# A turned merge, a freed buffer as a ring place, and a small router table ahead of the rest of the router

## The reference, cut to what matters

```python
y_r, y_n = rwkv7_time_mix(...), nsa_mix(...)                 # each 512 tokens x 512
gates  = sigmoid(zg).reshape(B, T, 2, D)
merged = gates[:, :, 0] * (y_r @ p_rwkv) + gates[:, :, 1] * (y_n @ p_nsa)
h  = h + gt1 * (merged @ w_out)
u2 = rmsnorm(h, norm_ffn_g) * (1 + sc2) + sh2
# router: best group of 4, two best of its 8 experts, weights from both softmaxes
# experts: every expert's tokens, in blocks;  hid = silu(x @ w_gate[e]) * (x @ w_up[e]);  hid @ w_down[e]
h  = h + gt2 * hier_moe(u2, ...)
return rmsnorm(h, norm_final_g)
```

## Time and profile before

| | us |
|---|---|
| time, median of 3 runs | 1168.78 (1166.61 to 1171.31) |
| profiled execution, time | 1164.38 |
| profiled execution, span | 1162.5 |
| PE busy | 1064.9 (92%) |
| DVE busy | 474.9 (41%) |
| ACT, POOL busy | 203.0, 161.3 |
| DMA, mean over the span | 258 GB/s |

### The profile page before, as it was taken

How to read it: one execution, slowest core, us unless ns; L and a number is a source line. 1 busy time by engine, 2 the same in 40 slices (tenths; PEclk the granted TensorE clock), 3 DMA queues, 4 the chain that set the end, 5 groups by cost and what they waited for, 6 DMA issues and landing times.

```text
span 1162.5 us, 13892 instructions
## 1 busy us (share of the span) xinstructions
PE 1064.9 (92%) x5547; PEld 512.2 (44%) x5547; DVE 474.9 (41%) x831; ACT 203.0 (17%) x444; POOL 161.3 (14%) x225
## 2 busy tenths in 40 slices
PE   5999999999998898998999859999999989989796
PEld 4443344455445565776444524443333333333332
DVE  4663446563082653457424451122222313212165
ACT  4011114332102564232101200000000000000003
POOL 4100001141200444212000010100000000000321
PEclk8999999999999999999999979999999989999999
DMA  9933427324936300100874489999999999999993
GB/s 351 385 108 109 162 92 283 116 90 154 253 107 157 109 1 23 44 3 2 339 278 184 161 320 402 426 429 425 429 425 427 427 428 426 426 427 426 426 401 128
DMA packets 73377, 299.62 MB, mean 258 GB/s; under 512 B 21422, under 2 KB 27920, under 8 KB 60384
## 3 DMA queue, kind: packets, MB, share of 16 engines
q1 hardware_dynamic: 59776, 278.00, 60.7%
q0 software_dynamic: 6912, 15.46, 3.5%
q10 hardware_dynamic: 6624, 5.26, 1.5%
HBM read 288.13 MB, written 17.84 MB: 263 GB/s over the span
## 4 chain that ended last, share of the span: by engine, by line
PE 43%; DMA 4%; DVE 2%; issue 2%; ACT 1%; SPq 0%; POOLq 0%; ACTq 0%; DVEq 0%
PE ps L2776 18%; PE ps L2802 9%; PE ps L2693 5%; PE ps L2754 5%; DMA ring<-in_moe_w_down_dram 3%; PE ps L2644 3%; PE ps L2737 1%; PE ps L2786 1%; ACT hdT L2268 1%; PE ps L2660 1%; PE ps L2875 1%; DMA zrT<-u_dram,slots 0%; DVE mg L2601 0%; PE ps L2672 0%; PE ps L2632 0%
## 5 line engine op out<-in xcount | busy, mean ns | idle before, releaser
L2776 PE MATMUL ps<-ring,zrT 128*64 128x512 f32 x624 | 189.6, 608 | 14.8 <-issue 13.9
L1058 PE MATMUL ps<-ring,uT 128*128 128x512 f32 x384 | 169.9, 597 | 0.6 <-PE ps L976 0.6
L2776 PEld LDWEIGHTS ps<-ring,zrT 128*64 128x64 f32 x624 | 60.5, 140 | 135.8 <-issue 135.8
L1047 PE MATMUL ps<-uT,ring 128*128 128x512 f32 x256 | 116.2, 611 | 2.0 <-DVE uT L709 1.4
L2802 PE MATMUL ps<-ring,hdT 128*64 128x512 f32 x336 | 99.2, 594 | 12.7 <-ACT hdT L2268 11.4
L1058 PEld LDWEIGHTS ps<-ring,uT 128*128 128x128 f32 x384 | 71.4, 190 | 86.8 <-issue 86.3
L2484 DVE TENSOR_TENSOR cst<-cst,ps 128x512 f32<-128x512 f32 x16 | 11.0, 688 | 167.5 <-PE ps L2776 167.5
L1047 PEld LDWEIGHTS ps<-uT,ring 128*128 128x128 f32 x256 | 49.0, 195 | 66.1 <-issue 64.8
L2517 DVE TENSOR_TENSOR h<-h,ps 128x512 f32<-128x512 f32 x64 | 44.0, 688 | 61.3 <-PE ps L2754 60.6
L2496 DVE TENSOR_TENSOR zrT<-ps,mod 128x512 f32<-128x512 f32 x32 | 22.1, 692 | 99.2 <-PE ps L2802 99.2
L2802 PEld LDWEIGHTS ps<-ring,hdT 128*64 128x64 f32 x336 | 33.2, 137 | 65.6 <-issue 65.6
(11 more groups left out here) (446 smaller groups left out, 1447.7 us busy)
## 6 DMA issues: line engine op xcount, KB each, us to landing
ring<-in_moe_w_gate_dram SPq DMA_DIRECT2D x19, 2048.0 KB, 34.4
ring<-in_moe_w_up_dram SPq DMA_DIRECT2D x18, 2048.0 KB, 35.2
ring<-in_moe_w_down_dram SPq DMA_DIRECT2D x18, 2048.0 KB, 35.4
ring<-in_w_in_dram SPq DMA_DIRECT2D x8, 2048.0 KB, 12.5
ring<-in_w_ada_dram SPq DMA_DIRECT2D x8, 2048.0 KB, 8.6
ring<-in_w_ada_dram SPq DMA_DIRECT2D x16, 512.0 KB, 13.4
zrT<-in_moe_w_gate_dram SPq DMA_DIRECT2D x4, 2048.0 KB, 35.8
zrT<-in_moe_w_up_dram SPq DMA_DIRECT2D x3, 2048.0 KB, 38.5
```

What stands on the lines that cost most here:

```text
L1047: ins = pe.matmul(ps[:, n % 4, :], slot(name, KD, w)[:, k, c0:c0 + P], uT[:, k, :], start=(k == 0), stop=(k == KD - 1))
L1058: ins = pe.matmul(ps[:, n % 4, :], uT[:, k, P * i:P * i + P], w, start=(k == 0), stop=(k == KD - 1))
L2776: ins = pe.matmul(ps[HALF * r:HALF * r + HALF, "gu".index(kind), :], xgT[:, k, HALF * r:HALF * r + HALF], w[r][:, k, :], start=(k == 0), s ...
```

## The change

Merge: the products are made the other way round (weights held still, tokens streamed), so that they come out already turned; DVE writes `mgT` at once, eight tiles of 128 columns by 512 tokens, and `mg`, its transposes and ACT's copies are gone. `gates_dram` is stored turned too, and the gate loads become eight of 0.5 MB, the later four after `m_mg` 1 to 4. The two p_nsa products of tiles 6 and 7 move ahead of the wait for y_r's transposes. `mg`'s room becomes `tenth`, ring place 7, first in `order`, with no condition. Place 6 now waits for the four rows in memory, since the second half of the `u2` buffer lies in it. Place 0 is given back after the first output product.

Router: DVE makes a small table of the 16 pairs alone (`at_expert`, `at_rank`, 16 small products, `r_pt`), from which come the first 16 `slots`. The rest of the router follows, with DVE's copy `tokens(0)` put in its middle. The large table (`tables`) is made after product g of pair 0, the weights' table (`weight_table`) in the middle of its product u.

```diff
-        ztiles += [("zg", f"zg{b}{j}", i, 0) for j in range(2) for b in range(2) for i in range(NT)]
+        ztiles += [("zg", f"zg{b}{j}", i, P * i) for j in range(2) for b in range(2) for i in range(NT)]
-                        if kind == "T":
+                        if kind in ("T", "zg"):
...
-        order = (1, 2, 0, 9, 5, 3, 4, 6, 7, 8)
+        order = (7, 1, 2, 0, 9, 5, 3, 4, 6, 8)
...
                 elif turns == 0 and s_ == 6:
-                    eng.wait_ge(n2_u, NT)
-                elif turns == 0 and s_ == 7:
                     eng.wait_ge(n2_row, 16 * NT)
...
-                else:
+                elif (turns, s_) != (0, 7):
                     eng.wait_ge(unit_free[s_], turns + fills[s_])
...
+                def gate(n):
+                    wait(sp, m_mg, n - 3)
+                    sp.dma_start(gates[:, n % 4, :, :], gates_dram[:, P * n:P * n + P, :].rearrange("b p n -> p b n"))\
+                        .then_inc(m_gt[n % 4], 16)
+
+                for n in range(4):
+                    gate(n)
                 load_units(sp, index["wo0"], index["wo1"])
-                sp.wait_ge(m_mg, 2)
-                gate(2)
+                gate(4)
+                gate(5)
                 load_units(sp, index["wo1"], NU)
-                sp.wait_ge(m_mg, 4)
-                gate(3)
+                gate(6)
+                gate(7)
                 sp.dma_start(h[:, :, :], ...)
...
@@ DVE, merge @@
-                    dve.tensor_tensor(mg[:, i, cols], tmps[:, 0, :], tmps[:, 1, :], ALU.add).then_inc(m_mg, 1)
+                    dve.tensor_tensor(mgT[:, n, :], tmps[:, 0, :], tmps[:, 1, :], ALU.add).then_inc(m_mg, 1)
...
@@ DVE, router, after ohb @@
+                TS(at_expert[:, :, :, 0:NPAIR], oh_half, C("place"), None, ALU.mult).then_inc(r_ex, 1)
+                for j in range(2):
+                    TT(at_expert[:, NT * j:NT * j + NT, :, NPAIR:], oh_half[:, NT * j:NT * j + NT, :, :], ...)
+                dve.wait_ge(r_rk, 1)
+                link(TT(t64[:, :, :, :], oh[:, :, :, :], over_both(ps[:, 1, 0:NT * E]...), ALU.mult))
+                link(dve.tensor_reduce(R_, t64[:, :, :, :], AX, ALU.add))
+                TT(at_rank[:, :, :], C("iota")[:, 0:HALF]..., rx..., ALU.is_equal).then_inc(r_ra, 1)
+                link(dve.tensor_copy(cnt[:, :], ps[:, 1, NT * E:NT * E + E]))
+                link(TS(M_, R_, float(HALF), None, ALU.is_ge))
+                dve.wait_ge(r_pt, 1)
+                link(TS(hi[:, 0:NPAIR], ps[:, 2, NPAIR:2 * NPAIR], -float(P), float(T), ALU.mult, ALU.add))
+                dve.tensor_tensor(slots[:, 0:NPAIR], hi[:, 0:NPAIR], ps[:, 2, 0:NPAIR], ALU.add).then_inc(r_sl, 1)
...
+                tokens(0)
...
                 dve.tensor_copy(w_part[:, 2, :, :], w_blk[:, :, :]).then_inc(r_wp, 1)
+                dve.wait_ge(r_tab, 1)
+                link(TS(hi[:, :], ps[:, 2, NBLK:2 * NBLK], -float(P), float(T), ALU.mult, ALU.add))
+                link(dve.tensor_tensor(slots[:, NPAIR:NBLK], hi[:, NPAIR:NBLK], ps[:, 2, NPAIR:NBLK], ALU.add))
...
@@ PE, merge @@
-                def turned(m):
...
+                for n in (6, 7):
+                    nsa_product(pe, n, n - 2)
+                pe.wait_ge(m_yTe, NT)
+                for n in range(KD):
+                    if n >= 4:
+                        pe.wait_ge(m_mg, n - 3)
+                    for k in range(4):
+                        ins = pe.matmul(ps[:, n % 4, :], slot("p_rwkv", 4, D)[:, k, P * n:P * n + P], yrT[:, k, :],
+                                        start=(k == 0), stop=(k == 3))
+                    ins.then_inc(m_p, 1)
...
@@ PE, output product @@
+                            if n == 0:
+                                pe.wait_ge(m_mg, k + 1)
...
+                        if n == 0:
+                            pe.sem_inc(unit_free[0], 1)
...
@@ PE, router and experts @@
+                for n in range(2 * NT):
+                    for half in range(2):
+                        ins = pe.matmul(ps[HALF * half:HALF * half + HALF, 2, 0:2 * NPAIR], at_rank[:, n, :],
+                                        at_expert[:, n, half, :], start=(n == 0), stop=(n == 2 * NT - 1))
+                ins.then_inc(r_pt, 1)
...
                     for k in range(KD):
+                        if (kind, b, k) == ("u", 0, 4):
+                            weight_table()
...
                     product("g", b)
                     if b == 0:
+                        tables()
```

More of the change, by code:

```diff
@@ L148, in stream_units @@
     units.append(("p_nsa", [(HD * g, HD, (4, D), p_nsa[g]) for g in range(2)]))
[L149 removed]
+    wo = A["w_out"][0].rearrange("(k p) n -> p k n", p=P)
     for h in range(2):
@@ L1880, in build @@
         mgT = uT[:, :, :]
-        gates = more[0][:, R2 - 1 - RP, :].rearrange("p (a b n) -> p a b n", a=2, b=2)
+        gates = more[0][:, R2 - 1 - RP, :].rearrange("p (a b n) -> p a b n", a=4, b=2)
         grow2 = zrT[:, 8:10, :].rearrange("p a n -> p (a n)")
[L1883 to L1887, removed]
+        u2 = (zrT[:, 10:12, :].rearrange("p a n -> p (a n)"), mod[:, 1, :])
+        (m_yT, m_yTe, m_p, m_mg, m_o, m_h, m_dve, m_h0, m_g, m_wr, m_lg, m_bias, m_wg) = (
+            sem(f"m_{n}") for n in "yT yTe p mg o h dve h0 g wr lg bias wg".split())
+        m_gt = [sem(f"m_gt{n}") for n in range(4)]
         n2s = alloc(top, "n2s", [P, 4, NT])
@@ L1915, in build @@
         at_place = rb("hidden", "at_place", [P, 2 * NT, P], BF16)
+        at_rank = rb("hidden", "at_rank", [P, 2 * NT, HALF], BF16, over=0)
+        at_expert = rb("rows", "at_expert", [P, 2 * NT, 2, 2 * NPAIR], BF16, over=0)
         w_part = rb("rows", "w_part", [P, 3, 2 * NT, NBLK], BF16)
@@ L1920, in build @@
         hi = rb("rows", "hi", [P, NBLK])
-        at_block = rb("turned", "at_block", [P, 2 * NT, 2, NBLK], BF16)
+        at_block = rb("weights", "at_block", [P, 2 * NT, 2, NBLK], BF16)
         lg = rb("turned", "lg", [P, NT, NG + E])
@@ L1925, in build @@
         ohb = rb("turned", "ohb", [P, NT, E], BF16)
-        rank = rb("turned", "rank", [P, NT, E])
-        cnt, nov, ovi, ovs = (rb("turned", n, [P, E]) for n in ("cnt", "nov", "ovi", "ovs"))
+        cnt, nov, ovs = (rb("turned", n, [P, E]) for n in ("cnt", "nov", "ovs"))
+        ovi = rb("weights", "ovi", [P, E])
         kst = rb("turned", "kst", [P, 2 * NT, NS])
@@ L1938, in build @@
         nst = rb("low", "nst", [P, E, NS])
-        hi2 = rb("low", "hi2", [P, NBLK])
+        hi2 = rb("weights", "hi2", [P, NBLK])
         r_a, r_b, r_e, r_oh, r_rk, r_dve, r_at, r_tab, r_sl, r_ov, r_row = (
             sem(f"r_{n}") for n in "a b e oh rk dve at tab sl ov row".split())
+        r_ex, r_ra, r_pt = (sem(f"r_{n}") for n in ("ex", "ra", "pt"))
         xg = zrT[:, 12:14, :].rearrange("p a n -> p (a n)")
@@ L1992, in branch, with out_bank @@
                 return nsa_kept(n)
-            return ps[:, 6 + n if b and n < 2 else 2 * (n % 2) + b, :]
+            return ps[:, (6 + n if n < 2 else n - 2) if b else n % 4, :]
+        def out_bank(n):
+            return (6, 4, 5)[n % 3]
         def expert_slot(s_, k):
@@ L2229, in _ @@
                         .then_inc(m_yTe, 1)
[L2230 to L2234, removed]
                 def h_out(i):
@@ L2309, in _ @@
                 link = Chain(dve, m_dve)
[L2310 to L2313, removed]
+                for n in range(KD):
+                    dve.wait_ge(m_gt[n % 4], 16 * (n // 4 + 1))
                     dve.wait_ge(m_p, n + 1)
@@ L2812, in _ @@
                     if b == 0:
-                        pe.wait_ge(r_wp, 1)
-                        for m in range(3):
-                            for n in range(2 * NT):
-                                ins = pe.matmul(ps[:, 3, 2 * NBLK:3 * NBLK], at_place[:, n, :], w_part[:, m, n, :],
-                                                start=(m + n == 0), stop=(m == 2 and n == 2 * NT - 1))
-                        ins.then_inc(r_wt, 1)
+                        tables()
                     if b - 1 in ADDED:
```

152 lines of the change are left out of this document (65 added, 87 removed).

## The result

| | before | after |
|---|---|---|
| time, median of 17 runs each, us | 1165.43 (1160.97 to 1171.31) | 1173.78 (1169.52 to 1178.98) |
| ratio, 95% interval | | 1.0073 [1.0058, 1.0089] |
| profiled execution, time and span, us | 1164.38 and 1162.5 | 1177.46 and 1175.5 |

The change costs 8.35 us.

What follows compares the result with a forecast made beforehand. The prediction took the weights' stream, timed by the end of u of pair 0, as the bound. Terms +2.3 + 1.5 + 2.0 + 0.6 = +6.4 gave 1170.8 us for the profiled execution, 1175.2 as median; range 1165 to 1181.

Steps and rivals of the forecast that it cites:

- What bounds the kernel: Expert stage runs at the weights' pace; the end hangs on u of pair 0 ending, about 702 us.
- Merge on PE: Merge: four transpose groups removed and two p_nsa products covering the wait for ACT; -4.5 us in all.
- Merge on SP and the first fall: Router loads behind the later `h` load: PE stands 4.8 us at the biases, then half clock costs 2.0.
- The small table: Router: first slots 6.4 us earlier, gather and transposes as before, so pair 0's rows are turned 6.4 us earlier.
- The rest of the router: ACT's copy of half 4 to 7 waits for `r_wp`, so PE stands about 7.9 us in mid g.
- The second fall: Clock falls again after PE's stand in the middle of g; +2.0 us (0 to 2.8).
- the tables between g and u: The large table's sixteen products, moved between products g and u of pair 0; about +0.6 us.
- The ring place: Filling ring place 7 earlier only moves a load from one queue gap to another; costed at nothing.
- Small loads in time: Rival: biases start at 591.2, no first stand or clock fall; sum -0.4, 1168.4 us; chance 0.18.
- no hold on g: Rival: `r_wp` early enough for ACT's copy, no 7.9 wait or second clock fall; -3.5, 1165.3 us; chance 0.10.
- Bytes alone: Rival: weight bytes alone set the end, one more load ahead shortens the stream; -4.9, 1163.9 us; chance 0.07.
- Half-size gate loads: Rival: split gate loads hold the queue, 8.8 us more ahead of `h`; +15.2, 1184.0 us; chance 0.05.

Runs made afterwards that it cites:

- e3: Changed kernel with the ring order of the kernel before (place 7 in ninth position); ratio to before 1.0129.
- e9: Changed kernel, ACT's copy not behind `r_wp`, small router loads before gate load 4, POOL's memset early, place 6's load after the first gather; 0.9932 of before.
- e8: Changed kernel with ACT's copy of half 4 to 7 not behind `r_wp` and small router loads ahead of gate load 4; ratio to before 0.9975.
- e11: Changed kernel's merge and ring place with before's router order, and small router loads ahead of gate load 4; ratio to before 0.9956.
- e5: Changed kernel with POOL's memset ahead of the last row's wait and place 6's load held until the first gather landed; ratio to before 1.0030.
- e10: Changed kernel with only the load into place 6 held until the first gather has landed; ratio to before 1.0040.
- e1: Changed kernel, but ACT copies half 4 to 7 before waiting for `r_wp`; ratio to before 1.0010.
- e7: Changed kernel with before's ring order and the loads into places 6 and 7 held until the first gather has landed; ratio to before 1.0044.
- e4: Merge, loads and ring of the changed kernel with the router order of the kernel before; ratio to before 1.0008.
- e6: Changed kernel with eight more unused products on PE ahead of its wait for the second half of g's rows; ratio to before 1.0071.
- e2: Changed kernel with the five small router loads issued ahead of gate load 4; ratio to before 1.0056.

## Why the prediction was right, and where it was not

- *What bounds the kernel.* Right for this change. In eleven profiles the time from load 12 to the end is 460.2 to 461.3 us wherever load 12 lies; e3 with 461.7 and e9 with 462.6 are the exceptions. A slip of reading without effect: the load issued at 596.33 is the fifth, and it is the sixth that goes out after the 60 us.
- *Merge on PE, -4.5.* Measured -4.0 (M to W in e8, e9 and e11 against 101.8).
- *Merge on SP and the first fall, +4.8 and +2.0.* Right in its place, too large for an ordinary execution. `h` went out 5.8 us later (forecast 6.1). The profile after has 3.73 of stand and 2.9 of fall, 6.6; the five other kernels with the same loads 2.58 to 3.10 and 1.7, and 4.3 us in M to W. (The recovery times behind the 2.0 were misread by 0.4 us: the figures 0.69 and 0.82 of the earlier trace rows put the clock's return 5.8 and 3.3 us after PE had resumed, which is 2.9 and 1.7 of lost work; the 2.0 still lies between.) Two router loads stuck, for 5.86 and 3.30 us, where one had stuck for 10.66.
- *The small table, -6.4.* This is the term that failed. "Gather 4.47 and transposes 1.17 as before" left out that place 6's load, which I had moved behind the last row of `u2`, now goes out right ahead of the gather. X gained 2.6 us instead of 6.4: the gather took 7.13, the transposes 1.97, and POOL's memset came late. The memset was late because the last row of `u2` was in memory only 1.8 us earlier behind W than before (16.1 against 17.9), not the forecast's 4.9. With no load issued just ahead of the gather W to X falls by 6.7 to 7.4 (e5, e9, e10), so the table's own price was right, and a little low. This term is also why load 12 went out later than the forecast's 708 to 709: 10.3 us later behind M than before, not 6.4.
- *The rest of the router, +7.9.* Right: the second half of g at X + 12.25 (forecast 12.3). Without the hold X to L is 8.0 us less (e1), which is the 7.9 and the second fall's 1.6 less the 1.4 that g then loses at half clock.
- *The second fall, +2.0, and the tables between g and u, +0.6.* The second half of g took 5.17 us instead of 3.58, so 1.6; the sixteen small products 0.54.
- *The ring place, 0.* Wrong, though not by bytes. The old order costs 5.6 us (e3), by way of the gather, which the forecast held apart from the ring; with the gather free it costs nothing that can be told (e7 against e10).
- *The rivals.* Small loads in time, and no hold on g: neither came about, PE stood at both places. The two stands are the loss, as e8 shows by taking them away; e1 alone came to +1.2 us and not to the forecast's -3.5, since that sum carries the same gain of 6.4 at X. Bytes alone: out by e7, and back in sight in e9 only. Half-size gate loads: `h` would have gone out 8.8 us later still; a load of 512 KB took 5.6 us in the median against 6.0 for the 1,024 KB of before. The rule of the Trainium skill ("DMA: Bandwidth & Descriptors", section "Bandwidth") to batch to 1 MiB or more cost nothing to break that these rows show, with several loads in flight. The fixed 2.0 us that the forecast set beside it is that page's fit for transfers issued from GpSimd, and the gate loads are issued by SP.

An estimate of the sum for an ordinary execution, from the stages: M to W +0.2 (102.0, the mean of e1, e4, e5, e6 and e10, less 101.8), W to X -2.6, X to L +10.1, behind L +0.4, together +8.1; the medians say +8.35. The forecast's +6.4 had 2 us too much in the first stage and 4 us too much gain in the second.

## What to carry to other kernels

When a load moves behind an event, look at what else that event sets free: here the last row of `u2` released a load of 2 MB and a gather on which everything waited, and the load went first. And a step that is put off for the sake of an earlier one keeps its old waits; look for whoever waits on its semaphore (ACT's `r_wp`) before counting the gain. A change that loses can hold a gain: with two waits, a memset and five loads moved, the same merge and table are 0.7% faster than before.

## What the hardware showed that was not expected

The first gather took 3.9 to 4.5 us with no load of weights issued in the 2.5 us ahead of it (before, e4, e5, e7, e9, e10, e11; mean 4.2), 6.5 to 7.2 with one (after, e1, e2, e6, e8; mean 7.0), and 10.88 with two (e3): 2.8 us for the first load and 3.9 for the second, where a load takes 4.9 of the DMA engines' time. In the profile after, the DMA queues (packets, MB, share of 16 engines) show that the gather mostly waits for its place. From its issue (679.8) to 684.2 SP's queue (q1) moves nearly all of the load and POOL's (q0) not one packet; then the gather's 144 packets move within 2.5 us:

```profile
q1 hardware_dynamic: 108, 1.77, 95.1%
...
q0 software_dynamic: 144, 0.28, 29.1%
q1 hardware_dynamic: 20, 0.07, 6.5%
```

In e10, with no load ahead, they start within 1.8 us of the issue. In e3 none moves for the first 4.3 us either, and then they take 6 us, beside SP's second load (144 and 158 packets in 686.4:692.6). The Trainium skill ("DMA: Bandwidth & Descriptors", section "Queues, rings and completion order") has each DMA engine serve its queues by turns, a whole packet at a time. The rows of e3 agree for the second load; for the first they show no turns, and whether a load is one such packet the trace does not tell.

The granted clock moved the common first half of the program (up to M) by up to 8.6 us between executions, more than the whole effect of the change, so two profiles could be compared only stage by stage.
